# PEER expert mixer: 192 prompt tokens through every expert, 128 tokens through gathers summed on DVE

## The reference

```python
q = (xb @ wq).reshape(TOK_BLOCK, PEER_HEADS, D_KEY)
s1, s2 = scores of both halves of q against 128 keys each
v1, i1 = lax.top_k(s1, 16); v2, i2 = lax.top_k(s2, 16)
cand = v1[..., :, None] + v2[..., None, :]
cidx = i1[..., :, None] * 128 + i2[..., None, :]
best, sel = lax.top_k(cand, 16)
eidx = take_along_axis(cidx, sel)
gate = softmax(best)
act = gelu(einsum('thkd,td->thk', u_tab[eidx], xb))
out = einsum('thk,thkd->td', gate * act, v_tab[eidx])
```

## Time and profile before

| what | us |
|---|---|
| median of 3 runs | 2993.45 |
| lowest and highest run | 2988.42, 2997.27 |
| the profiled execution | 2988.82 |
| its span (first to last instruction) | 2987.0 |
| granted TensorE clock, mean of the span | 0.872 |
| `stage_experts` of the first layer, from 652.35 to 1500.25 | 847.90 |
| `stage_experts` of the second layer, from 2119.50 to 2959.03 | 839.53 |

### The profile page before, as it was taken

How to read it: one execution, slowest core, us unless ns; L and a number is a source line. 1 busy time by engine, 2 the same in 40 slices (tenths; PEclk the granted TensorE clock), 3 DMA queues, 4 the chain that set the end, 5 groups by cost and what they waited for, 6 DMA issues and landing times. The chain is left out here.

```text
span 2987.0 us, 22085 instructions
## 1 busy us (share of the span) xinstructions
PE 2323.2 (78%) x7282; PEld 1188.1 (40%) x7282; DVE 1530.7 (51%) x3784; ACT 614.9 (21%) x1453; POOL 953.0 (32%) x917
## 2 busy tenths in 40 slices
PE   6957456888778787778889987798778787777876
PEld 4634123553333333333357672365433333333333
DVE  1043221386676766645313563625766667774553
ACT  2134242121122211111121121102222221221112
POOL 0000673014444444444201120001244454444441
PEclk8977677998998989899889988799898889999988
DMA  6654785259999999999723204315599999999993
GB/s 266 235 199 170 247 294 170 100 220 384 419 413 395 404 400 388 403 406 413 303 91 114 88 1 169 127 57 224 205 407 394 402 401 414 409 410 401 418 415 142
DMA packets 121907, 860.24 MB, mean 288 GB/s; under 512 B 15346, under 2 KB 17977, under 8 KB 27457
## 3 DMA queue, kind: packets, MB, share of 16 engines
q0 software_dynamic: 102400, 721.47, 60.4%
q1 hardware_dynamic: 19393, 137.36, 12.1%
HBM read 845.65 MB, written 13.18 MB: 288 GB/s over the span
## 5 line engine op out<-in xcount | busy, mean ns | idle before, releaser
L1980 POOL DMA_INDIRECT expin_uv<-in_peer_uv_dram,expin_expert x432 | 523.5, 1212 | 999.6 <-PE exp_acc L2055 565.9
L2104 DVE CUSTOM_DVE_ANT_0 expin_uv<-expin_uv,expin_htok 128x1024 f32<-128x1024 f32 x432 | 523.8, 1227 | 398.2 <-DMA expin_uv<-in_peer_uv_dram,expin_expert 394.1
L2054 PE MATMUL exp_acc<-expin_uv,exp_diag 128*128 128x512 f32 x864 | 512.8, 678 | 256.0 <-ACT exp_diag L2071 255.7
L2055 PE MATMUL exp_acc<-expin_uv,exp_diag 128*128 128x512 f32 x864 | 485.5, 646 | 0.0
L2054 PEld LDWEIGHTS exp_acc<-expin_uv,exp_diag 128*128 128x128 f32 x864 | 174.2, 212 | 521.7 <-ACT exp_diag L2071 338.2
L1980 POOL DMA_INDIRECT exp_uv<-in_peer_uv_dram,expin_expert x208 | 248.4, 1194 | 365.3 <-PE exp_acc L2055 257.4
L2104 DVE CUSTOM_DVE_ANT_0 exp_uv<-exp_uv,expin_htok 128x1024 f32<-128x1024 f32 x208 | 251.6, 1228 | 173.8 <-DMA exp_uv<-in_peer_uv_dram,expin_expert 171.6
L2054 PE MATMUL exp_acc<-exp_uv,exp_diag 128*128 128x512 f32 x416 | 243.7, 670 | 113.2 <-ACT exp_diag L2071 113.2
L2063 ACT ACTIVATE exp_act<-exp_dots 128x4 f32<-128x4 f32 x160 | 32.9, 206 | 1219.8 <-DVE exp_dots L2104 1219.8
L2055 PEld LDWEIGHTS exp_acc<-expin_uv,exp_diag 128*128 128x128 f32 x864 | 182.9, 212 | 243.6 <-issue 243.6
L2055 PE MATMUL exp_acc<-exp_uv,exp_diag 128*128 128x512 f32 x416 | 230.7, 638 | 0.0
(11 more groups left out here) (362 smaller groups left out, 2467.4 us busy)
## 6 DMA issues: line engine op xcount, KB each, us to landing
norm_w<-in_ada_pk_dram SPq DMA_DIRECT2D x12, 2048.0 KB, 8.2
attp_w<-in_ada_pk_dram SPq DMA_DIRECT2D x12, 2048.0 KB, 8.1
ssd_in_w<-in_ssd_w_in_pk_dram SPq DMA_DIRECT2D x20, 1024.0 KB, 4.8
peer_q_w<-in_peer_wq_pk_dram SPq DMA_DIRECT2D x16, 1024.0 KB, 5.0
ab_in_w<-in_ab_w_in_pk_dram SPq DMA_DIRECT2D x10, 1024.0 KB, 10.2
state_h<-in_state_ssmT_dram SPq DMA_DIRECT2D x8, 1024.0 KB, 4.8
out_ssm_sampleT_dram<-state_h SPq DMA_DIRECT2D x8, 1024.0 KB, 3.9
ssd_out_w<-in_ssd_w_out_pk_dram SPq DMA_DIRECT2D x4, 2048.0 KB, 10.0
```

The costliest lines, as they stand in the source:

```text
L1980: pool.indirect_dma_start(self.slot(g)[:], None, self.table, bass.IndirectOffsetOnAxis(ap=self.expert[:, g:g + 1], axis=0)).then_inc(self. ...
L2054: pe.matmul(acc[t % 2][0][:], diag[g % (2 * GRP)][:], slot(g)[:, D:D + 512], start=False, stop=False, skip_group_check=True)
L2055: pe.matmul(acc[t % 2][1][:], diag[g % (2 * GRP)][:], slot(g)[:, D + 512:2 * D], start=False, stop=False, skip_group_check=True).then_inc( ...
L2104: dve.tensor_tensor_reduce(slot(g)[:, 0:D], slot(g)[:, 0:D], x.htok[:, t, :], 1.0, 0.0, ALU.mult, ALU.add, dots[:, i % 2, k:k + 1]).then_i ...
```

## The change

The 320 tokens are split. Tokens 0 to 191 (`TD = 192`, all of the prompt) no longer gather. `stage_experts` runs three parts for them. In the U part every U table row is streamed (64 loads of 1 MB on SP's queue, 3 buffers) and PE makes, for each of 128 blocks of 128 experts, eight matmuls of 192 columns; ACT applies gelu and keeps all 16384 activations of the 192 tokens in SBUF (`big`). In the weight part the gate weights of 4 tokens at a time (48 groups) are built as a 128 by 128 matrix each: POOL makes `hot_i`, DVE and ACT half of `hot_j` each, PE multiplies the two, and DVE multiplies the result into the activations; weights of experts that were not chosen are zero. In the V part every V table row is streamed the same way and PE sums in PSUM. Tokens 192 to 319 keep gathers, now 128 per layer in a ring of 5 slots, and no matmul: `dot` on DVE as before, `weigh` on ACT, `add` on DVE (scale the V half and add it to `otok`). 46 of these 128 steps are placed in the U part (between the remaining 14 turns and after them), 8 in the weight part (`breaks`, after groups 5, 11, ... 47) and 74 in the V part. In `stage_peer_q` 8 transposes a layer are left of 24.

```diff
-RING = 12
-AHEAD = 8
+RING = 5
+STREAM = 3
+TD = 192
...
     def gather(self, pool, g):
+        if g >= P:
+            return
+        pool.wait_ge(self.chosen, g // TOPK + 1)
         if g >= RING:
-            pool.wait_ge(self.mixed, g - RING + 1)
+            pool.wait_ge(self.summed, g - RING + 2)
...
+    def weigh(self, act, g):
+        act.wait_ge(self.dotted, g + 1)
+        act.activation(self.acts[:, g % 2:g % 2 + 1], self.dots[:, g % 2:g % 2 + 1], ACT.Gelu).then_inc(self.acted, 1)
...
+        act.mul(self.ws[:, g % 2:g % 2 + 1], self.acts[:, g % 2:g % 2 + 1], self.gate[:, g:g + 1]).then_inc(self.weighed, 1)
+
+    def add(self, dve, g):
+        dve.wait_ge(self.weighed, g + 1)
+        dve.wait_ge(self.summed, g + 1)
+        dve.scalar_tensor_tensor(out=self.otok[:], in0=self.slot(g)[:, D:2 * D], scalar=self.ws[:, g % 2:g % 2 + 1], in1=self.otok[:],
+                                 op0=ALU.mult, op1=ALU.add).then_inc(self.summed, 1)
...
+    chunk = A[:].rearrange("p (j t) -> p j t", t=TD)
+    by_token = A[:].rearrange("p (j t) -> p t j", t=TD)
...
+                for n in range(2 * pairs):
+                    if STREAM <= n < pairs + STREAM:
+                        sp.wait_ge(umade, 2 * (n - STREAM + 1))
+                    if n >= pairs + STREAM:
+                        sp.wait_ge(used, n - pairs - STREAM + 1)
...
+                pool.wait_ge(umade, NK)
+                pool.wait_ge(tkept, 8)
+                for k in range(groups):
+                    if k >= 2:
+                        pool.wait_ge(wmade, k - 1)
+                    for u in range(4):
+                        t = 4 * k + u
+                        ins = pool.tensor_scalar(hot_i[k % 2][:, u, :], m.iota[:], iT[:, t:t + 1], None, ALU.is_equal)
+                    ins.then_inc(is_made, 1)
+                    if k in breaks:
+                        x.gather(pool, breaks[k] - 1 + RING)
...
+                    for c in range(KC):
+                        ins = pe.matmul(ps[j % 6][:, 0:TD], wt[n % STREAM][:, u * D + c * P:u * D + (c + 1) * P], m.hT[:, c, 0:TD],
+                                        start=(c == 0), stop=(c == KC - 1))
+                    ins.then_inc(umade, 1)
...
+                    for u in range(4):
+                        ins = pe.matmul(psw[k % 2][:, u * NK:(u + 1) * NK], hot_i[k % 2][:, u, :], hot_j[k % 2][:, u, :], start=True, stop=True)
+                    ins.then_inc(wmade, 1)
...
+                pe.wait_ge(wdone, groups)
...
+                        ins = pe.matmul(acc[c // 2][:, (c % 2) * TD:(c % 2 + 1) * TD], wt[n % STREAM][:, u * D + c * P:u * D + (c + 1) * P], chunk[:, j, :],
+                                        start=False, stop=False, skip_group_check=True)
...
+                    act.activation(chunk[:, j, :], ps[j % 6][:, 0:TD], ACT.Gelu).then_inc(ukept, 1)
...
+                        act.activation(apart_j[:, u, :], m.iota[:], ACT.Abs, bias=njT[:, t:t + 1], scale=1.0).then_inc(apartd, 1)
...
+                        ins = act.activation(hot_j[k % 2][:, 2 + u, :], apart_j[:, u, :], ACT.Relu, bias=gT[:, t:t + 1], scale=ngT[:, t:t + 1])
...
+                for k in range(groups):
+                    dve.wait_ge(wmade, k + 1)
...
+                    v = by_token[:, 4 * k:4 * k + 4, :]
+                    dve.tensor_tensor(v, v, psw[k % 2][:].rearrange("p (u y) -> p u y", y=NK), ALU.mult).then_inc(wdone, 1)
+                    if k + 2 < groups:
+                        columns(k + 2)
+                    if k in breaks:
+                        step(breaks[k])
```

More of the change, by code:

```diff
@@ L1942, in _ @@
                 keep(w.blocks - 1)
+                for g in range(x.STEPS_Q):
+                    x.weigh(act, g)
             @block.vector
@@ L1953, in _ @@
                     choice.experts_of(dve, x, j)
+                dve.wait_ge(hkept, 2)
+                for g in range(x.STEPS_Q):
+                    x.dot(dve, g)
+                    if g:
+                        x.add(dve, g - 1)
 class Expert:
+    STEPS_Q = 0
+    STEPS_U = 46
+    STEPS_W = 8
     def __init__(self, nc, m, a, layer):
@@ L2091, in _ @@
-                spread(groups - 1)
-                end(2)
+                for j in range(NK):
+                    act.wait_ge(umade, j + 1)
+                    if j == free_from:
+                        act.wait_ge(lastd.sem, 1)
+                    act.activation(chunk[:, j, :], ps[j % 6][:, 0:TD], ACT.Gelu).then_inc(ukept, 1)
+                    for kind, k in due.get(j, ()):
+                        if kind == "turn":
+                            choice.exp(act)
+                        else:
+                            x.weigh(act, k)
@@ L2094, in _ @@
+                for g in range(after_w, P):
+                    x.weigh(act, g)
             @block.vector
@@ L2129, in _ @@
-                groups = turns * per
-                for i in range(groups):
-                    j, k = i // per, i % per
-                    dot(i)
-                    if i:
-                        weigh(i - 1)
-                    if j + EARLY < turns and k == 0:
-                        choice.best_sums(dve, x, j + EARLY)
-                    if j + EARLY < turns and k == 1:
-                        choice.experts_of(dve, x, j + EARLY)
-                    for t in (1, 2):
-                        if i == first[t] * per + 3:
-                            end(t - 1)
@@ L2142, in _, with step @@
-                weigh(groups - 1)
-                end(2)
+                def step(g):
+                    x.dot(dve, g)
+                    if g:
+                        x.add(dve, g - 1)
+                for kind, k, _ in items:
+                    if kind == "turn":
+                        choice.best_sums(dve, x, k)
+                        choice.experts_of(dve, x, k)
+                        if k == TURNS - 1:
+                            lastd.by(dve.nop())
+                    else:
+                        step(k)
```

406 lines of the change are left out of this document (231 added, 175 removed).

## The result

The changed kernel takes 3018.98 us (median of 20 runs, 3012.02 to 3026.96), the kernel before 2994.45 in as many: a ratio of 1.0081, 95% interval 1.0065 to 1.0098. It is slower by 24.5 us where 64 less were forecast. The two profiled executions have spans of 3018.9 and 2987.0.

What follows compares the result with a forecast made beforehand. DMA bytes were taken to bound the kernel. Per layer U 337, weight part 128 and V 347 sum to 812 against 843.7 us, 64 saved in both layers: 2929 us, range 2865 to 3020.

Steps and rivals of the forecast that it cites:

- the 818 of the old bytes: Expert stage before the change: 335.5 MB of gathers a layer at 0.41 cannot take much less than 818 us.
- U and V parts: Streamed table parts of each layer: U 337 us, paced by PE; V 347 us, PE and DMA ending nearly together.
- the holes: Weight part: at seven places a step delays the next group through gather and comparisons, 7.5 us each.
- quiet groups: Weight part, groups without a step: 1.7 us each, 41 of them a layer; ends 1.4 and 2.0.
- the ends: Weight part, outside the groups: 6 us for turned choices, their copies on ACT and the first comparisons.
- PE's own term: Weight part, PE's eight instructions a group: 0.9 us at full clock, 1.6 near the lower level of 1.2 GHz.
- The strided product: Slower rival, weight part: DVE's product at 4 ns an element takes 2.2 us and sets the pace; kernel 3046; chance 0.17.
- Late tables: Rival, mainly V part: table loads get under 203 GB/s, PE waits; 20 to 30 us a layer, 2970 to 2990; chance 0.16.
- Cheap groups: Rival, weight part: groups take 1.4 us and the eight places 6, part 105, kernel 2883; chance 0.15.
- ACT and DVE in step: Rival: late DVE stops ACT among its evictions, then PE; at 15 us a layer, kernel 2960; chance 0.07.
- the outer end of the weight part: Slow end of the weight part's forecast: groups of 2.4 us and holes of 8.5, 165 us instead of 128.
- three signs against the sum: Profile signs that would prove the sum wrong: product over 1.7 us, table loads over 10 us, weight part under 105.

Runs made afterwards that it cites:

- e7_three_pool: Changed kernel with no steps in the weight part (54 in U), POOL making three comparisons of a group and DVE the fourth: 2883.62 us.
- e2_no_breaks: Changed kernel with the eight steps of the weight part moved to the U part (54 there): 2921.29 us.
- e3_gather_later: Changed kernel with POOL issuing each weight-part step's gather two groups later: 2967.37 us.
- e6_both_later: Changed kernel with each weight-part step's gather on POOL and its gelu and gate on ACT issued two groups later: 2949.53 us.
- e10_two_ops: Changed kernel with POOL's comparison written as two operations, times 1.0 and then equal to the column: 3060.26 us.
- e11_two_ops_no_breaks: Changed kernel with POOL's comparison written as two operations and no steps in the weight part (54 in U): 2970.30 us.
- e5_half_pool: Changed kernel with POOL making only two of the four comparisons of a group (some weights wrong): 2953.66 us.

## Why the prediction was wrong

**What bounds the kernel before** was read rightly: fewer bytes did pay. With the weight part mended (e7_three_pool) the kernel is 112 us faster, and from the first matmul of U to the last of V its layers take 780.9 and 787.9 us, less than the 818 of the old bytes. (The kernel before has 320 gathers a layer, as the prediction counts; the 640 in its description are those of both layers.)

**U and V parts** held: 340.8 and 341.9 for 337, 340.2 and 343.7 for 347. So did the 0.161 us a matmul instruction (335.8 us over 2048 are 0.164), the hidden weight loads, and the cover of DVE and ACT beside them.

**The step that failed** is in the weight part: "POOL has four comparisons of 128x128: 0.295 to 0.319 for the nearest rows, though one is of 64 columns, so 1.2 to 1.6". It is 0.60 each, 2.4 a group. The rows were of other forms: one a mask, the other a product and sum, 374 ns had it had 128 columns. No row showed this form, and the two nearest agreed so well that I took them for bounds. The pace became 2.36 instead of 1.7 (40 x 0.66 = 26 us a layer). With half of the comparisons, so at the 1.2 us a group that I had put, the part took 148 and the kernel 2954. That is faster than before, on the forecast's side: POOL's price was enough to turn the sign. It was not the only term of this weight. Each of the holes took 10.1 us instead of 7.5 (18 us a layer, 7 of them the comparisons' price once more); without the steps alone the kernel was faster too (2921), and with the packed product alone as fast as before (2996).

**The remaining 20 us a layer** of the run with half of the comparisons are smaller terms: quiet groups of 1.89 in the mean instead of 1.7 (8 us), holes of 8.8 instead of 7.5 (9), the ends (4). The holes' mechanism was right, even to its sequence; missed were the 0.78 us until POOL goes on after the add, the comparisons in it (2.42 instead of 1.4) and the product. ACT's wait for the dot, behind which its own columns queue, I had left out; it hid under POOL's until that was taken away. PE's own term was low too, without effect: eight matmuls take 1.05 us in the earlier trace rows, not 0.9, and here 1.13 at the full clock and 2.08 at the lower one, where 0.9 and 1.6 were put.

**The strided product**, my rival on the slower side, had the right part of the kernel but the wrong engine; that it named the very pace that was measured (2.36) is chance. The product takes 1.29, between my 1.03 and the 1.7 from which it decides. 1.03 is what one strided side costs (1.025 and 1.032): the row of a strided read the earlier trace rows says nothing of a strided write, and the product has both.

**The other rivals.** Late tables did not come: 6.8 and 9.8 us a load, 408 GB/s in V. Cheap groups did not come. ACT and DVE in step did not come in the changed kernel, but did in small with 54 steps in U (8.5 and 11.5 us of PE's waits for ACT in e2_no_breaks and e7_three_pool).

**The range and the signs.** The measured time lies 1 us inside the upper end of the range (3020), which stood for the strided product and late tables; that is luck, since neither was the cause. No rival gave POOL's comparisons a higher price, though the outer end of the weight part had a pace of 2.4 (there 6 + 41 x 2.4 + 7 x 8.5 make 164, not 165; and the dots of the earlier trace rows stand 2.49 us apart, not 2.48; neither matters). None of the three signs against the sum came (a product over 1.7 us, loads over 10 us, a part under 105), while the sum was 48 and 50 us short in the weight part: a sign for a long part was missing.

## What to carry to other kernels

An operation that no row shows in its own form (the operations, how many, constant or column, the engine) has no price from rows of other forms that happen to agree; on an engine that would set a pace, give it a rival of its own. Work that waits for a far event (a gather's free slot, a weight's dot) should not stand in the queue of an engine that feeds another: issue it where the event is long past, on every engine that handles it. When a stage is paced by one of several engines working in parallel, compute the next pace behind it as well; here the gains stopped at DVE's pace, 1.7 us with two comparisons on POOL and 1.9 to 2.0 with three.

## What the runs showed of the hardware

POOL's elementwise price depends on the form more than on the width. The product and sum cost (374 - 317) / 64 = 0.89 ns a column, the comparison with a column (602 - 440) / 64 = 2.5. The Trainium skill, "GPSIMD Engine Reference", section "3.1 Elementwise — side-by-side cycle accounting", gives 1.03 cycles an element for k of up to 2, read here as up to two operations; at the 1.2 GHz of its section "1. Specifications" that is an estimate of 0.86 ns. The first form agrees. The comparison takes three times as much, with one operation; here the measurement decides.

A comparison that runs beside DVE's dot or add takes 1.33 to 1.86 us instead of 0.60, in the two runs where they meet (44 in e3_gather_later and e6_both_later; 11 others, which overlap one by 0.55 us at most, took 0.59 to 0.71). Beside the product, which reads PSUM and SBUF, its median there is 593 ns. The Trainium skill, "SBUF — State Buffer", section "SBUF: two separate sides", says that a DVE operation with two SBUF inputs and a GpSimd operation shut each other out for a whole instruction; dot and add have two, the product one. The 44 and the product agree with it; why the 11 short overlaps cost nothing is not shown.

The granted clock of the weight part was higher in the runs whose groups came faster, and at one pace higher without steps. It was 0.51 at 2.79 and 2.84 us a group (e10_two_ops, e11_two_ops_no_breaks; eight matmuls in 2.08 us in all 96 groups, the 1.2 GHz level), 0.65 and 0.61 at 2.35 with steps (the change), 0.73 and 0.72 at 2.33 without (e2_no_breaks), 0.75 at 1.73 with steps (e5_half_pool), and 0.92 and 0.89 at 1.93 and 2.03 (e7_three_pool; 1.13 us in 72 of 96 groups, the 2.4 GHz level).
